# Multiplying constant masks into idle PSUM banks at nine calls of a two-model transformer kernel

## What is computed

```python
def hybrid_layer(x, ...):                       # first model, 2 layers
    u = rms_norm(x, g_mix_pre) @ w_in           # 1024 -> 3200
    y = concat(chunk_attention(...), conv_module(...), retention(...))
    x = x + rms_norm(y @ w_out, g_mix_post)
    f = square(relu(rms_norm(x, g_mlp_pre) @ w_up)) @ w_down     # 1024 -> 4096 -> 1024
    return x + rms_norm(f, g_mlp_post)

for l in range(2):                              # second model
    x = x + 0.5 * swiglu(rmsnorm(x, ffn1_norm[l]), ...)          # 1024 -> 2816 -> 1024
    h = rmsnorm(x, mix_norm[l])
    o = concat(mla_attention(...), nsa_attention(...), stick_breaking_attention(...))
    x = x + o @ w_out[l]
    x = x + 0.5 * swiglu(rmsnorm(x, ffn2_norm[l]), ...)
return rmsnorm(x, final_norm)
```

## Time and profile before

| | |
|---|---|
| median of 3 runs | 3617.1 us (3615.09 to 3623.82) |
| span of the profiled execution | 3618.4 us |
| PE busy | 3444.5 us (95%), 15812 products |
| PE weight load busy | 2672.3 us (74%) |
| DVE, ACT, POOL busy | 1645.6, 1223.6, 207.6 us |
| mean granted clock of TensorE | 0.976 of full |
| PE in the chain that ended last | 90% |
| read from HBM | 285.25 MB, 79 GB/s over the span |

### The profile page before, as it was taken

How to read it: one execution, slowest core, us unless ns; L and a number is a source line. 1 busy time by engine, 2 the same in 40 slices (tenths; PEclk the granted TensorE clock), 3 DMA queues, 4 the chain that set the end, 5 groups by cost and what they waited for, 6 DMA issues and landing times.

```text
span 3618.4 us, 45576 instructions
## 1 busy us (share of the span) xinstructions
PE 3444.5 (95%) x15812; PEld 2672.3 (74%) x15812; DVE 1645.6 (45%) x2137; ACT 1223.6 (34%) x1821; POOL 207.6 (6%) x247
## 2 busy tenths in 40 slices
PE   7988999898899999999999999999999999999998
PEld 5656888675578886888665678887888776578886
DVE  3755443566354335343345554434443443654433
ACT  3334122332422234232344433233332344442232
POOL 1200000021010000000002210000000001200000
PEclk9999999899999999999999999999999999999999
DMA  5213332231243222333221033332332221023331
GB/s 156 65 35 74 96 99 94 75 89 40 64 94 99 93 87 82 99 93 99 70 59 30 25 93 93 99 98 78 98 95 97 79 72 35 12 78 99 99 94 63
DMA packets 416615, 289.24 MB, mean 80 GB/s; under 512 B 23520, under 2 KB 394380, under 8 KB 416216
## 3 DMA queue, kind: packets, MB, share of 16 engines
q1 hardware_dynamic: 413592, 280.74, 26.6%
q0 software_dynamic: 2736, 4.58, 0.9%
q10 hardware_dynamic: 144, 2.10, 0.2%
HBM read 285.25 MB, written 2.13 MB: 79 GB/s over the span
## 4 chain that ended last, share of the span: by engine, by line
PE 90%; DVE 4%; ACT 3%; issue 3%; DMA 1%; DVEq 0%; POOL 0%; ACTq 0%; SPq 0%; POOLq 0%
PE bank L1698 27%; PE bank L1699 26%; PE bank L1700 26%; PE bank L1708 2%; PE bank L1785 1%; PE bank L1831 1%; PE bank L1807 1%; PE bank L1875 1%; ACT whi L864 1%; PE bank L2125 0%; PE bank L2123 0%; PE bank L1738 0%; PE bank L1909 0%; DVE stat L1325 0%; PE bank L2114 0%
## 5 line engine op out<-in xcount | busy, mean ns | idle before, releaser
L1698 PE MATMUL bank<-hh,whi 128*128 128x512 f32 x2848 | 1144.7, 402 | 62.8 <-DVE hl L1251 22.7
L1699 PE MATMUL bank<-hl,whi 128*128 128x512 f32 x2848 | 1123.9, 395 | 0.0
L1700 PE MATMUL bank<-hh,wlo 128*128 128x512 f32 x2848 | 1123.0, 394 | 0.0
L1234 DVE TENSOR_TENSOR wlo<-raw,whi 128x1024 fp32r<-128x1024 f32 (+2 forms) x536 | 645.2, 1204 | 457.1 <-ACT whi L864 443.0
L1698 PEld LDWEIGHTS bank<-hh,whi 128*128 128x128 f32 x2848 | 544.8, 191 | 209.7 <-issue 40.0
L864 ACT ACTIVATE whi<-raw 128x1024 fp32r<-128x1024 f32 (+2 forms) x536 | 547.6, 1033 | 252.2 <-PE bank L1700 239.6
L1699 PEld LDWEIGHTS bank<-hl,whi 128*128 128x128 f32 x2848 | 544.8, 191 | 115.9 <-issue 5.3
L1700 PEld LDWEIGHTS bank<-hh,wlo 128*128 128x128 f32 x2848 | 543.8, 191 | 116.4
L1698 PE MATMUL bank<-fshi,whi 128*128 128x512 f32 (+2 forms) x1364 | 537.2, 394 | 0.1
L1700 PE MATMUL bank<-fshi,wlo 128*128 128x512 f32 (+2 forms) x1364 | 525.6, 385 | 0.0
L1699 PE MATMUL bank<-fslo,whi 128*128 128x512 f32 (+2 forms) x1364 | 525.5, 385 | 0.0
(11 more groups left out here) (222 smaller groups left out, 2361.2 us busy)
## 6 DMA issues: line engine op xcount, KB each, us to landing
raw<-in_ffn_w_gate SPq DMA_DIRECT2D x88, 512.0 KB, 3.8
raw<-in_ffn_w_up SPq DMA_DIRECT2D x88, 512.0 KB, 3.8
raw<-in_ffn_w_down SPq DMA_DIRECT2D x88, 512.0 KB, 3.4
raw<-in_w_in SPq DMA_DIRECT2D x82, 512.0 KB, 3.8
raw<-in_w_up SPq DMA_DIRECT2D x64, 512.0 KB, 4.1
raw<-in_w_down SPq DMA_DIRECT2D x64, 512.0 KB, 3.3
raw<-in_w_out SPq DMA_DIRECT2D x16, 512.0 KB, 4.0
raw<-in_w_in SPq DMA_DIRECT2D x16, 256.0 KB, 3.4
```

What stands on the lines that cost most here:

```text
L1234: dve.tensor_tensor(slot3(wlo, s, m), slot3(raw, s, m), slot3(whi, s, m).bitcast(F32), ALU.subtract).then_inc(c.lo_done.sem, 1)
L1698: pe.matmul(o, wh, ah, start=start, stop=False)
L1699: pe.matmul(o, wh, al, start=False, stop=False)
L1700: return pe.matmul(o, wl, ah, start=False, stop=stop)
```

## The change

A helper `keep_warm(n, bk)` on PE multiplies `identb` by the first 512 columns of `m_sb` into bank `bk`, n times. Nobody reads the result. It is called at nine places, each in the body of a loop over two layers, so 222 products are added in all. Four of the calls have a wait of their own ahead of them. No other engine's program is changed.

```diff
+WARM_MIX1, WARM_SUM, WARM_POST, WARM_FF, WARM_MIX2, WARM_STICK = 26, 5, 14, 12, 14, 9
...
+            def keep_warm(n, bk):
+                for _ in range(n):
+                    pe.matmul(bank[:, bk, :], identb, m_sb[:, 0:S], start=True, stop=True)
...
             def down(...):          # its end, only in the first model
                 else:
+                    pe.wait_ge(c.y0.sem, c.y0.at(l, 2))
+                    keep_warm(WARM_SUM, 0)
                     norm_added(c, l, a)
...
             with pe.Fori(0, LAYERS) as l:                    # first model
+                keep_warm(WARM_MIX1, 7)
                 first_two(c, b, l, [gr["unit"] for gr in b["order"][:2]], [gr["bank"] for gr in b["order"][:2]], 0)
...
                 out_product(c, b, l)
+                pe.wait_ge(c.y0.sem, c.y0.at(l, 1))
+                keep_warm(WARM_SUM, OUT_BANK)
                 norm_added(c, l, A1_POST, OUT_BANK)
+                pe.wait_ge(c.rn_ln.sem, c.rn_ln.at(l, 2))
+                keep_warm(WARM_POST, OUT_BANK)
...
                 down(c, b, l, n0 + T1, 0, T1, A1_MPOST, ...)
+                pe.wait_ge(c.rn_ln.sem, c.rn_ln.at(l, 4))
+                keep_warm(WARM_POST, 0)
                 norm(c, l, A1_NEXT, KT, bank[:, 0, :])
...
             with pe.Fori(0, LAYERS) as l:                    # second model
+                keep_warm(WARM_FF, 7)
                 mlp(l, 0, 0, A2_MIX, 0, None)
+                keep_warm(WARM_MIX2, 7)
                 first_two(c, b, l, [gr["unit"] for gr in b["order"][:2]], [gr["bank"] for gr in b["order"][:2]], 8)
...
                     elif s[0] == "z":
+                        if s[1] == 0:
+                            keep_warm(WARM_STICK, 7)
...
                 late_product(c, b, l)
+                pe.wait_ge(c.x_ready.sem, c.x_ready.at(l, KT + 5))
+                keep_warm(WARM_FF, 4)
                 mlp(l, b["wo"] + b["n_out"], T2, A2_NEXT, 19, A2_MLP)
```

## The result

| | before | after |
|---|---|---|
| median of four runs each | 3620.46 us (3615.09 to 3623.97) | 3601.07 us (3598.54 to 3603.08) |
| span of the profiled execution | 3618.4 us | 3596.7 us |
| PE busy | 3444.5 us | 3466.5 us |
| mean granted clock | 0.976 | 0.989 |

The ratio of the times is 0.994, 95% interval 0.9922 to 0.9958: faster by 19.4 us. PE is busy for longer than before, since it has 222 products more, and is done earlier all the same. First the page's busy times of the kernel after, which answer to the earlier trace rows; DVE, ACT and POOL read as before.

What follows compares the result with a forecast made beforehand. PE's stream, busy 95% of 3618.4 us, was taken to bound the kernel. Gains of 4.9 + 0 + 3.6 + 3.2 + 2.85 + 4.2 + 0 = 18.8 us gave 3599.6 profiled, 3598 as a median; range 3588 to 3612.

Steps and rivals of the forecast that it cites:

- The bound and the ceiling: PE busy 95% of the span; eleven half-clock stretches, 55.93 us busy, give at most 26.2 us at full clock.
- The stages behind the sums, scores and the late product: PE's work there returns to full clock: 4.9 us at first sums, 2.85 at first scores, 4.2 after late product.
- after the down product: 5 and 14 products before eight norm sums; the last square waits for DVE's x, so gain 0, cost 0.
- Before the mixer: 14 products fit the 3.79 us wait; the 3.41 us half-clock stretch is worth 1.6 us, twice, 3.2.
- the entry of the second model's first layer: 12 products fit the 3.06 us wait; a new 0.9 us wait for unit 1's low weights leaves gain 1.9 us.
- The jump of the loop: At second-layer entry of the first stage, PE pays 0 to 2.15 us; at 2.15 the 26 products overrun 1.1 us, absorbed.
- the entry of the second model's second layer: The batch of 12 begins 2.15 us later after a jump, still fits into 5.29 us: gain 1.7 us.
- What I took for the clock: Clock held everywhere except at the first stage's two entries, where 0 of 1.8 us each was taken.
- Half of it: Rival: clock falls at the 5+14 batches and one or two more, leaving 8 to 12 us: 3607 us; chance 0.28.
- More than that: Rival: both first-stage entries hold too, +3.6 us, and some attention-stage falls shift away: 3592 us; chance 0.13.
- The products don't count: Rival: the clock depends on data, mostly zero masks hold nothing, and batches overrun: 3629 us; chance 0.07.
- The slow side: Half-clock batches overrun at first stage's second entry, after the down product and at second model's entry: 12 us, 3629.

Runs made afterwards that it cites:

- a second set: The changed kernel itself, unedited, timed again as a control in another set of runs: 3597.0 us, ratio 0.993 to the kernel before.
- halved: Changed kernel with all batches at half their count (13, 3, 7, 6, 7, 5): 3601.52 us, ratio 0.9948 to the kernel before.
- without the fives: Changed kernel without its batches of 5 products at both calls, their waits kept: 3603.5 us, ratio 0.9951 to the kernel before.
- zero operand: Changed kernel with a tile of zeros as the products' moving operand: 3601.95 us, ratio 0.9946 to the kernel before.
- none at the first sum: Changed kernel without the 5 and 14 products and their waits after the first half of a first-model layer: 3606.59 us, ratio 0.9964 to the kernel before.
- 4: Changed kernel with other edges: some entry products moved ahead of the loops and their jumps, 20 ahead of the last transposes: 3598.43 us.
- 6: Changed kernel with two places more per layer: 13 products ahead of `rq1`, 16 ahead of the seventh score step: 3593.93 us.
- 1: Changed kernel with narrow products, each writing 16 columns instead of 512, same waits: 3619.46 us, ratio 0.9997 to the kernel before.
- doubled counts: Changed kernel with every batch at twice its count, 444 products: 3627.93 us, ratio 1.0019 to the kernel before.

## Why the prediction was right, and where it wasn't

The forecast was 3598 us as a median, in a range of 3588 to 3612, "faster" at 0.70. Measured were 3601.07 and, in a second set, 3597.0. By the profiled executions 21.7 us went where 18.8 were forecast. That the medians differ by 19.4 is closer than the working deserves: it is a sum with terms missed on both sides, below.

**The bound and the ceiling.** The reading that PE's stream sets the time and can only gain by the clock stands: 20.8 of the 21.7 us lie behind the calls, and with narrow products there is no gain.

**The price of an added product.** 0.216 us at full clock, below the 0.227 taken as the dear end. It changed nothing at the calls that fit.

**The stages behind the sums, scores and the late product.** 2.5, 2.85, 2.64 and 1.60 us were forecast; 2.54 and 2.46, 2.79, 2.57 and 1.61 were measured. The same working said 0 after the down product, because the last square waits for DVE: 0.05. Before the mixer 1.6 was forecast and 1.41 and 1.50 measured. DVE's tiles come 1.39 us apart there (its `hl` at 1737.13 and 1738.52), and PE, never idle, takes as long for six products; 48 starts took 11.21 us (1737.95 to 1749.16), 0.234 each and not 0.227, and these are the 0.2 us. At the entry of the second model's first layer the forecast wait for the low weights of unit 1 came: 0.63 us against 0.9, gain 2.1 against 1.9 (the rows give 1384.53 - 1382.51 = 2.0).

**The jump of the loop: the step that was mis-sized.** I had bounded what PE pays by ACT's row of 2.15 us, "between 0 and 2.15". PE paid 3.02 and 2.73 in the change, 2.6 to 3.3 in the other kernels without products ahead of the jump, once 4.96; only with products queued ahead of it 1.4 to 1.9 us of idle were left. The row of another engine was no upper bound. It shows in the first product of the first stage's second layer: forecast 1.1 us late, found 1.66 (702.93 us, a shift of 4.51 behind one of 6.17). As forecast, the stage behind absorbs that, and the clock held this time, so the stage gained 0.94 where I had put 0. In four other kernels with 26 products there it fell (the three at the end of the table, and with two places more): the entry ran from 1.9 us gained down to 2.2 us lost. So the price of the jump was the term that was mis-sized, by 0.9 us; one of the forecast's own signs of being wrong, a first product later than 2.2 us after the last norm sum, came true (the batch alone began 3.02 us after it). And I had reckoned with lateness alone there, not with a fall of the clock inside the batch.

| kernel | ahead of the jump | "issue", us | batch | entry's gain, us |
|---|---|---|---|---|
| other edges | 8 | 1.89 | 8 in 1.89 us | 1.9 |
| halved | none | 3.16 | 13 in 2.97 us | 1.7 |
| after | none | 3.02 | 26 in 5.77 us | 0.9 |
| without the fives | none | 3.28 | 26 in 7.46 us | -1.0 |
| zero operand | none | 3.05 | 26 in 8.71 us | -2.05 |
| none at the first sum | none | 3.29 | 26 in 8.68 us | -2.2 |

The same jump explains the entry of the second model's second layer: 0.96 us against 1.7. There nine of the twelve products ran at half clock, and the first product came 1.52 us later against before than the last norm sum.

**What I took for the clock.** I read an idle of 2.25 us as harmless and nothing shorter than 2.90 as a fall. The trace of before had shorter ones, in the attention stages:

```profile
200.29 0.50 PE L1698 MATMUL bank<-hh,whi 128*128 128x512 f32 x1 [1.80 <-DVE G L1465]
...
201.16:204.57 3.41, 3.41 (x10) 2.64 (x9) 2.10 (x3) 1.47 (x3) 0.00 (x0) 0.50 0.02 5
```

So a length read at one place was no bound for another. With idles of 2.6 and about 2.2 us left at the two entries of the first stage I took 0 of 1.8 us each there (1.9 by the rows: 721.31 - 719.4). They held in the change, with 1.85 us before the tile in the first layer; with 2.75 us (4) and 2.68 us (6) there the clock fell. The caution left 2.7 us of gain unforecast. With the 0.9 of the earlier first tile, and less the 0.7 forecast too much at the second model's second entry, this makes the 2.9 us by which the sum fell short.

**The rivals.** "Half of it", 0.28, named its mechanism rightly for one kernel: without the fives the clock falls at the 14 after the down product. Its price was overstated, since that place absorbs. "More than that", 0.13, came true for the first entries (1.77 and 0.94 us), not in the attention stages. "The products don't count" fell with zero operands, 3601.95 us. What the Trainium skill says of the peak-current limiter (TensorE: Matmul & The Clock Gate, Part 1, "Seeing it yourself"), that all-zero operands don't trip it, does not carry over to this gate: here a moving operand of zeros kept the clock at 1.00 like masks. That the gate looks at how busy PE is, as the same page of the Trainium skill has it, agrees with the narrow products (clock 0.976, as before).

**The slow side** was priced at 12 us for batches that overrun. The doubled counts are 31 us behind their control and still only 6 us slower than before, with a mean clock of 0.988 against 0.976.

## What to carry to other kernels

Where the busiest engine is TensorE and the granted clock falls behind its waits, products that nobody reads, put into those waits, can win back nearly half of the busy time found at half clock (0.468 of it at most, here), if they end before the awaited tile comes; look for what is late next, since a stage that ends with another engine gives nothing back. Rather leave some idle time than fill the wait (0.3 to 1.1 us did no harm here): half the products kept most of the gain, double the products cost more than all of it. At a loop's jump put some of the products ahead of the jump, and judge gains of under 4 us by the stretches of the trace, not by a median of four runs.

## What the runs showed that I had not expected

- PE's jump back over the body of a large loop leaves 2.6 to 3.3 us of "issue" with the queue empty, once 4.96, and 1.4 to 1.9 us with six or eight products queued ahead of it. They fill the time and don't shorten it: in 4 the eight started at 697.63, the first behind the jump at 701.42. The Trainium skill (Runtime: NRT & Kernel Launch, "Instruction fetch mechanics") says that a taken branch beyond the instructions at hand has to fetch its target before execution goes on; the rows fit that, but none shows a fetch in that time.
- An idle length doesn't decide a fall by itself. Within one kernel, 2.25 us left the clock up (before, 345.16) and 1.80 us was followed by a fall (200.29); in the halved kernel 2.29 us left it up (320.01) and 1.80 us was followed by a fall (1757.05). Without the fives, 2.17 us let it fall (681.54).
- The clock fell also where PE's records leave no gap. In the kernel before, PE is busy for all of these three windows of the second model's mixer, the middle one with 64-column products (33 records), and the clock falls behind them. Full windows don't mean full work there: a record of such a product lasts 0.28 us and the next starts after 0.11 us, while the 16-column products of 1 started 0.025 us apart.

```profile
1860.04:1863.45 3.41, 3.41 (x23) 2.91 (x22) 0.00 (x0) 0.93 (x3) 0.00 (x0) 1.00 0.16 48
1863.45:1866.86 3.41, 3.41 (x33) 3.41 (x32) 0.06 (x1) 3.35 (x5) 0.00 (x0) 1.00 0.02 5
1866.86:1870.28 3.42, 3.42 (x18) 3.36 (x19) 3.17 (x3) 2.88 (x5) 0.00 (x0) 0.50 0.26 61
```

- Why some falls come in one execution of a kernel and not in the next (that at 249.89 us; the halved kernel's range is 3598.92 to 3612.2) stays open.
